# Feed-forward products on 2x2 blocks, seven block products in place of eight

## The reference, cut to what matters

```python
def ffn_block(x, hist, p):
    hu = rmsnorm(x, p['norm_ffn']) @ p['w_up']                  # 1024 -> 2 x 2816
    hp = jnp.concatenate([hist.astype(hu.dtype), hu], axis=1)
    c = lax.conv_general_dilated(hp, p['conv_w'][:, None, :], (1,), 'VALID',
                                 dimension_numbers=('NWC', 'WIO', 'NWC'),
                                 feature_group_count=hu.shape[-1]) + p['conv_b']
    a, g = jnp.split(c, 2, axis=-1)
    return x + (jax.nn.silu(a) * g) @ p['w_down'], hp[:, -(CONV_W - 1):]   # 2816 -> 1024
```

## Time and profile before

| | us |
|---|---|
| median of the runs (1861.76, 1865.08, 1868.53) | 1865.08 |
| span of the profiled execution | 1862.2 |
| `w_out`, 942.35 to 1034.68 | 92.3 |
| norm, 1034.68 to 1051.95 | 17.3 |
| feed-forward loop, 1051.95 to 1793.0 | 741.1 |
| transposes of the last rows, 1793.0 to 1815.16 | 22.2 |
| last down products and final norm, 1815.16 to 1846.19 | 31.0 |
| results, 1846.19 to the end | 16.0 |

### The profile page before, as it was taken

How to read it: one execution, slowest core, us unless ns; L and a number is a source line. 1 busy time by engine, 2 the same in 40 slices (tenths; PEclk the granted TensorE clock), 3 DMA queues, 4 the chain that set the end, 5 groups by cost and what they waited for, 6 DMA issues and landing times. The chain is left out here.

```text
span 1862.2 us, 27167 instructions
## 1 busy us (share of the span) xinstructions
PE 1730.0 (93%) x10863; PEld 1490.2 (80%) x10864; DVE 942.1 (51%) x1593; ACT 564.6 (30%) x876; POOL 351.0 (19%) x288
## 2 busy tenths in 40 slices
PE   5999999969989998878979899999999999999988
PEld 4655788956555554547979899999999999999978
DVE  3356216776553444119231455655565566556544
ACT  4001115645443444211132332222232222222232
POOL 0000100042213121212125022222222222222210
PEclk8999999979999999797989899999999999999988
DMA  6312516412326134354040111211112112111102
GB/s 241 70 63 77 222 32 227 176 57 62 102 64 214 57 93 179 119 168 148 4 128 1 42 34 40 62 34 59 42 34 68 34 34 68 34 46 55 34 12 97
DMA packets 90684, 155.15 MB, mean 83 GB/s; under 512 B 15302, under 2 KB 68078, under 8 KB 88254
## 3 DMA queue, kind: packets, MB, share of 16 engines
q1 hardware_dynamic: 76736, 93.13, 15.6%
q0 software_dynamic: 13056, 59.77, 9.8%
q10 hardware_dynamic: 816, 1.18, 0.2%
HBM read 133.61 MB, written 24.83 MB: 85 GB/s over the span
## 5 line engine op out<-in xcount | busy, mean ns | idle before, releaser
L2455 PE MATMUL ps<-h_up,w_split 128*128 128x344 f32 x2112 | 399.5, 321 | 7.1 <-DVE h_rest L2617 5.2
L2627 DVE TENSOR_TENSOR xT<-ps,xT 128x688 f32<-128x688 f32 x352 | 228.2, 690 | 283.3 <-PE ps L2455 268.3
L2455 PEld LDWEIGHTS ps<-h_up,w_split 128*128 128x128 f32 x2112 | 345.0, 189 | 8.9 <-DVE h_rest L2617 4.2
L2455 PE MATMUL ps<-gated,wd_split 128*128 128x344 f32 x1584 | 258.3, 321 | 0.9 <-ACT last_row L2569 0.9
L2455 PEld LDWEIGHTS ps<-gated,wd_split 128*128 128x128 f32 x1584 | 251.0, 188 | 1.6 <-issue 1.1
L2455 PE MATMUL ps<-h_rest,w_split 128*128 128x344 f32 x1056 | 224.8, 321 | 0.4 <-ACT wd_split L2565 0.4
L2455 PEld LDWEIGHTS ps<-h_rest,w_split 128*128 128x128 f32 x1056 | 179.1, 189 | 0.7 <-ACT wd_split L2565 0.7
L2581 POOL TENSOR_TENSOR w_split<-w_raw,w_split 128x1024 fp32r<-128x1024 f32 x44 | 114.3, 2598 | 152.4 <-ACT w_split L2527 152.4
L2541 ACT ACTIVATE hu<-ps 128x1032 f32<-128x1032 f32 x44 | 45.4, 1033 | 314.5 <-PE ps L2455 314.5
L2635 DVE SCALAR_TENSOR_TENSOR cv<-hu,ccol,cv 128x1024 f32<-128x1024 f32 x88 | 129.5, 1472 | 16.4 <-ACT cv L2543 10.7
L1719 DVE TENSOR_REDUCE top<-ps 128x1 f32<-128x384 f32 (+4 forms) x124 | 71.1, 585 | 108.1 <-PE ps L1302 63.2
(11 more groups left out here) (459 smaller groups left out, 2576.4 us busy)
## 6 DMA issues: line engine op xcount, KB each, us to landing
w_raw<-in_w_up SPq DMA_DIRECT2D x44, 512.0 KB, 6.2
wd_raw<-in_w_down SPq DMA_DIRECT2D x22, 512.0 KB, 3.6
unit<-in_cache_kv_win POOLq DMA_DIRECT2D x16, 512.0 KB, 4.5
x_kept<-xT SPq DMA_DIRECT2D x1, 4128.0 KB, 25.2
xT<-x_kept SPq DMA_DIRECT2D x1, 4128.0 KB
xtok<-in_x_prompt SPq DMA_DIRECT2D x2, 2048.0 KB, 8.2
w_qu<-in_w_in SPq DMA_DIRECT2D x2, 2048.0 KB, 8.7
w_out_sb<-in_w_out SPq DMA_DIRECT2D x4, 1024.0 KB, 11.1
```

What stands on the lines that cost most here:

```text
L2455: mm = pe.matmul(k.ps[:, bank + c, 0:TG], w(wn), x(xn)[:, c * TG:c * TG + TG], start=start and m == 0, stop=stop and m == 2)
L2627: dve.tensor_tensor(x[:, part], k.ps[:, bank + part.start:bank + part.stop, 0:TG], x[:, part], ALU.add).then_inc(added, 1)
```

## The change

The feed-forward products are made on 2x2 blocks. Up: the 8 blocks of features fall into two halves of four, the 1032 rows into two halves of 516 (HT), and the two columns are the sides a and g of step f. Strassen's scheme (in Winograd's form) needs seven block products in place of eight, of sums and differences of blocks:

- The sums of activations `S1` to `S4` are made once, ahead of the loop (S1, S2, S4 by VectorE, S3 by GpSimd), with their splits. The sums of weights `V1` to `V4` are made by GpSimd in each step (`w_sums`, four of 512 elements), and their rests and those of the raw blocks in four operations (`w_low`, three of 1024 and one of 512).
- A product is 4 blocks x 3 passes x 2 groups of 258 rows = 24 matmuls; seven of them are a step, in the order `LATER`. Products that add up share two banks (`BANK`), and A12, S3, S4 continue what A11, S2, S1 opened.
- Product A11 is copied to `base` by ScalarE. VectorE reads six results in the order u2, c11, u3, c22, c21, c12 (line 2942, 2948, 2954, 2958, 2963, 2967) into `hu`, which holds half steps z of 1032 rows as before.
- The operands are x times gain only. The norm's factor of a row is applied when PSUM is read (c11) or right behind it (`scale`, line 2971), so three products of the first step run beside the norm's sums (line 2508, 2549).
- The gated rows are stored to HBM (`g_kept`) and x with them (`x_kept_again`). The down products follow after the loop: six chunks of one or two pairs of feed-forward blocks (`CHUNKS`), four sets of output columns dp in each, seven products in a set. GpSimd makes the sums and rests of the down weights (`wd_prepare`); the sums and rests of the gated rows are made by GpSimd for pair 0 and by VectorE, piece by piece between its reads, for the others (`g_piece`). In chunk 0 ScalarE copies five of seven products out (`copies`) and stores the last rows, transposed in between (`keep_last`); afterwards VectorE adds each into `acc` (`read`) and, later, x.
- The final squares are taken in the last chunk (`FINAL`), and summed by GpSimd. The loops of the feed-forward part are written out, with no loop on the chip.
- `w_out` loads its weights block by block, and writes its sums to HBM as well.

The core of the diff; TensorE first, then ScalarE, GpSimd, VectorE:

```diff
+    LATER = ((A11, B11), (S1, V1), (S2, V2), (A12, B21), (S3, V3), (A22, V4), (S4, B22))
+    BANK = {A11: 0, A12: 0, S2: 2, S3: 2, S1: 4, S4: 4, A22: 6}
+    OPENS, CONTINUES = (A11, S2, S1, A22), (A12, S3, S4)
...
+    DOWN = ((A11, D11, 0), (S2, D2, None), (S1, D1, 4), (A12, D21, 0), (S3, D3, None), (S4, D22, 4), (A22, D4, None))
...
+    COPIED = (R_A11, R_S2, R_S1, R_A12, R_A22)
...
+    LAST_GROUPS = {0: range(0, 5), 2: range(5, NL)}
+    FINAL = [(20 + dp, d, r) for dp in range(4) for d, r in ((dp + 4, R_S4), (dp, R_A22))]
...
+            def keep_gated(f):
+                sp.wait_ge(multiplied, f + 1)
+                sp.dma_start(g_kept[f], k.cv[:, 1]).then_inc(gated_out, 16)
...
+                if f:
+                    keep_gated(f - 1)
+                if f + 2 < NF:
+                    sp.wait_ge(done, at_done(f, A12))
+                    load_up(f + 2, 0)
+                    sp.wait_ge(done, 7 * f + 7)
+                    load_up(f + 2, 1)
...
-                up(f, 0, first, f * 8 - 1, {KD - 2: ((left, f * 2), (added, f * 16)), KD - 1: ((w_upper, f * 3 + 2), (w_rest, f * 3 + 2))})
-                pe.wait_ge(gated_rest, f)
-                down(0)
-                pe.wait_ge(left, f * 2 + 1)
...
+                        for c in range(2):
+                            mm = pe.matmul(k.ps[:, bank + c, 0:HQ], ws[f % 2][:, w, a, :], xs[block][:, a, c * HQ:(c + 1) * HQ],
+                                           start=(block in OPENS and a == 0 and m == 0),
+                                           stop=(a == 3 and m == 2), skip_group_check=block in CONTINUES)
+                mm.then_inc(done, 1)
...
+                if block == A11 and f == 0:
+                    pe.wait_ge(o_added, KD - 1)
+                elif block == A11:
+                    pe.wait_ge(took, 6 * (f - 1) + C_11)
+                elif block == S1 and f:
+                    pe.wait_ge(took, 6 * (f - 1) + C_12)
...
+                elif block == A12:
+                    pe.wait_ge(based, f + 1)
...
+                elif block == S3:
+                    pe.wait_ge(took, 6 * f + U_2)
...
+                elif block == S4:
+                    pe.wait_ge(took, 6 * f + C_22)
...
+                                mm = pe.matmul(k.ps[:, bank + h, 0:HQ], ws[n % 2][:, w, m, :], xs[slot][:, block, h * HQ:(h + 1) * HQ],
+                                               start=(r <= R_S1 and m == 0 and y == 0),
...
+                act.wait_ge(w_in[f % 2], 32 * (f // 2 + 1))
+                if f >= 2 and n == 0:
+                    act.wait_ge(done, 7 * (f - 1))
+                if n:
+                    act.wait_ge(w_sum, 4 * f + W_SUMS[n])
+                g = W_GROUPS[n]
+                act.activation(group(k.w_up[f % 2], g), group(k.w_raw[f % 2], g), ACT.Copy).then_inc(w_upper, 1)
...
+            def base(f):
+                act.wait_ge(done, at_done(f, A11))
+                if f:
+                    act.wait_ge(took, 6 * (f - 1) + U_3)
...
+                act.activation(pair(k.base[:]), two(0), ACT.Copy).then_inc(based, 1)
...
+                act.wait_ge(scaled, 2 * f + z + 1)
+                if f:
+                    if z == 0:
+                        act.wait_ge(multiplied, f)
+                    else:
+                        act.wait_ge(gated_out, 16 * f)
+                act.activation(k.cv[:, z], k.hu[:, z, 2:], ACT.Identity, bias=k.ccol[:, 3, z * NF + f:z * NF + f + 1],
+                               scale=k.ccol[:, 2, z * NF + f:z * NF + f + 1]).then_inc(begun, 1)
...
+            for f in range(NF):
+                if f:
+                    base(f)
+                    silu(f - 1)
+                if f < LAST:
+                    for n in range(4):
...
+                begin(f, 0)
...
+                begin(f, 1)
...
+                for r in COPIED:
+                    act.wait_ge(down, 7 * n + r)
...
+                    act.activation(pair(dst), two(bank), ACT.Copy).then_inc(copied, 1)
+                    if r == R_A11 and n == 0:
+                        silu(LAST)
+                    if r == R_S1 and n in LAST_GROUPS:
+                        for x in LAST_GROUPS[n]:
+                            keep_last(x)
...
+                    if dp < 2:
+                        for x in range(4):
+                            g_high(1 + dp, x)
...
+            def w_sums(f):
+                w = k.w_raw[f % 2]
+                pool.wait_ge(w_in[f % 2], 32 * (f // 2 + 1))
+                if f >= 2:
+                    pool.wait_ge(done, 7 * (f - 1))
+                raw = lambda b: w[:, b]
+                for n, (o, a, b, op) in enumerate(((V1, V3, B11, ALU.subtract), (V2, V1, B22, ALU.subtract),
+                                                   (V3, B22, V3, ALU.subtract), (V4, B21, V2, ALU.add))):
+                    if n:
+                        pool.wait_ge(w_sum, 4 * f + n)
+                    pool.tensor_tensor(raw(o), raw(a), raw(b), op).then_inc(w_sum, 1)
...
+            def w_low(f, n):
+                if n == 0:
+                    pool.wait_ge(w_sum, 4 * f + 4)
+                pool.wait_ge(w_upper, 4 * f + n + 1)
+                g = W_GROUPS[n]
+                pool.tensor_tensor(group(k.w_rest[f % 2], g), group(k.w_raw[f % 2], g), group(k.w_up[f % 2], g).bitcast(F32),
+                                   ALU.subtract).then_inc(w_split, 1)
...
+            for f in range(NF):
+                if f:
+                    note(f - 1, 0)
+                    note(f - 1, 1)
+                if f < LAST:
+                    w_sums(f + 1)
+                    for n in range(4):
+                        w_low(f + 1, n)
...
+                    dve.wait_ge(convolved, 2 * f)
+                    dve.wait_ge(begun, 2 * f)
+                dve.tensor_tensor(pair(hu[:, 1, T_1]), two(2), pair(k.base[:]), ALU.add).then_inc(took, 1)
...
+                dve.tensor_tensor(pair(hu[:, 0, T_1]), two(0), pair(k.factor[:, 0:HT]), ALU.mult).then_inc(took, 1)
...
+                dve.tensor_tensor(pair(hu[:, 0, T_2]), two(2), pair(k.base[:]), ALU.add).then_inc(took, 1)
...
+                dve.tensor_tensor(pair(hu[:, 1, T_2]), two(4), pair(hu[:, 0, T_2]), ALU.add).then_inc(took, 1)
...
+                dve.tensor_tensor(pair(hu[:, 0, T_2]), two(6), pair(hu[:, 0, T_2]), ALU.add).then_inc(took, 1)
...
+                dve.tensor_tensor(pair(hu[:, 1, T_1]), two(4), pair(hu[:, 1, T_1]), ALU.add).then_inc(took, 1)
...
+            def scale(f, z, part, signal):
+                half = slice(0, HT) if part == T_1 else slice(HT, TOK)
+                ins = dve.tensor_tensor(hu[:, z, part], hu[:, z, part], k.factor[:, half], ALU.mult)
+                if signal:
+                    ins.then_inc(scaled, 1)
...
+            for f in range(NF):
+                if f:
+                    u2(f)
+                    gate(f - 1)
...
+                c11(f)
+                u3(f)
+                c22(f)
+                c21(f)
+                dve.wait_ge(took, 6 * f + C_21)
+                scale(f, 0, T_2, True)
+                scale(f, 1, T_2, False)
+                tap(f, 0, 0)
+                c12(f)
+                dve.wait_ge(took, 6 * f + C_12)
+                scale(f, 1, T_1, True)
+                tap(f, 0, 1)
+                tap(f, 1, 0)
+                tap(f, 1, 1)
...
+                    dve.tensor_tensor(raw(o), raw(a), raw(b), op).then_inc(g_sum, 1)
...
+                    dve.tensor_tensor(group(k.g_rest[s], g), group(k.g_raw[s], g), group(k.g_up[s], g).bitcast(F32), ALU.subtract
+                                      ).then_inc(g_split, 1)
...
+                dve.tensor_tensor(pair(dst), two(down_bank(n, DOWN[r - 1][2])), pair(dst), ALU.add).then_inc(joined, 1)
...
+                    read(n, r)
+                    if c < end and (dp > 0 or r >= 6) and pieces:
+                        g_piece(*pieces.pop(0))
...
+                    dve.wait_ge(x_in, 16 * d + 16)
+                    dve.wait_ge(*read_by(n, R_A22))
+                    dve.tensor_tensor(k.acc[:, d], k.acc[:, d], k.x_again[:], ALU.add).then_inc(x_joined, 1)
+                    dve.wait_ge(x_joined, d + 1)
```

972 lines of the change are left out of this document (617 added, 355 removed).

## The result

The changed kernel takes **1860.2 us** (median of 19 runs, 1852.5 to 1865.2) against 1864.8 in the runs beside it: a ratio of 0.9977, 95% interval 0.9966 to 0.9988. So it is faster by 0.23%, less than the 0.3% that I had called measurable. The forecast was 1849, 0.86% faster. The profiled execution has a span of 1856.7 us, 3.5 under its median, where before it was 1862.2.

What follows compares the result with a forecast made beforehand. TensorE, busy 93% of the span, was taken to bound the kernel. Terms from w_out on summed to 904 us against 919.9, 16 less: span 1846, plus 2.9 to the median, 1849; range 1795 to 1912.

Steps and rivals of the forecast that it cites:

- The matmul: Feed-forward matmuls on TensorE: 120 ns each at 258 columns, 5544 of them in 665 us, 85 us less than before.
- Rivals 4 and 5: Feed-forward matmuls: narrow ones bring nothing, +380 us (chance 0.01); or a matmul's fixed part goes, 1809 us (chance 0.05).
- The lock: Up loop: VectorE and GpSimd take turns at SBUF, 20.6 us of lock time a step against TensorE's 20.2.
- my layout: One up step laid out: u2 ends at 13.45 us, stalls before S1 0.4 and S3 1.45, step 22.2 us.
- The rest: Stages from the start of w_out to the span's end, summed term by term: 904 us against 919.9 before.
- w_out, 3 us: w_out: 92.3 us as now, plus 3 us for waits at d = 6 and 7, range 0 to 12.
- Five chunks, 22 us of stalls: Down stage after its first chunk: 201.6 us of matmuls plus 22 us of stalls, range 5 to 45.
- Tail, 5.2 us: Final read, square, 9 sums and root after the down stage: 5.2 us for the 9.3 before.
- 21 steps x 22.2: Up loop after its first step: 21 steps of 22.2 us, 466 us in all.
- The first chunk: First chunk of the down stage: ScalarE's serial work sets its pace, 54 us plus 8 for the clock, 62; 50 to 80.
- Within 0.3%: Whole kernel: its time changes by no more than about what a measurement can tell; chance 0.09.
- rival 3: Down stage: ScalarE's chain in the first chunk at 80 and VectorE's pieces at 30, +26, so 1875 us; chance 0.10.

Runs made afterwards that it cites:

- e1: Changed kernel with GpSimd's eight operations on the up weights cut to 8 elements each in the loop, output not the reference's: 1833.8 us, one run.
- e11: Changed kernel with GpSimd's first sum of 512 elements made twice in every step: ratio 1.0119 to the kernel before the change.
- e10: Changed kernel with the two notes of a step (10 elements each) moved from GpSimd to ScalarE: ratio 0.9985 to the kernel before the change.
- e14: Changed kernel with edits combined: w_out order, sample taps once, notes on ScalarE, first down chunk's buffers and order, pieces spread, final squares early: 1826.9 us, ratio 0.9771.
- e6: Changed kernel with the a side's second tap and the gate moved behind the next step's u2, and silu behind the weight copies: ratio 1.0244 to the kernel before.
- e2: Changed kernel with the taps of the eight sample rows made once, beside w_out: ratio 0.9949 to the kernel before the change.
- e3: Changed kernel with w_out's history transposes ahead of its first product and GpSimd's first up-weight sums and rests spread out: ratio 0.9943 to the kernel before.
- e4: Changed kernel with ScalarE making the next set's upper down weights ahead of this set's copies in the first down chunk: ratio 0.9982 to the kernel before.

## Why the prediction was wrong, point by point

**The matmul was right.** 120 ns at 258 columns was taken, and 120.7 measured where nothing waits (e1). Rivals 4 and 5 are out. The Trainium skill (TensorE: Matmul & The Clock Gate, Back-to-back issue gap) would have 110 for it by the rule that the prediction used, which the page gives for the isolated gap; the measurement decides.

**The lock was right, and its price a step a little high.** Forecast were a step of 22.2 us, a wait ahead of S3 for u2 and one ahead of S1 for c12. It is 21.4, with the wait ahead of S3 alone. In my layout u2 ended 13.45 us into the step; it ends at 12.6. The four collisions laid out ahead of it are there, at 1.0 to 1.1 us each in place of 1.15, and c12 ends at 2.6 and not at 3.2, in time for S1.

**What sets the step stays open in part.** e1 shows that it is GpSimd's operations beside VectorE that make it longer than 20.3 us. Two pictures are left of how. One is a sum: in the changed kernel an operation of VectorE with only SBUF operands, or one of GpSimd, runs for 20.7 of 21.4 us a step (by the timeline of 14 steps), close to the 20.6 estimated, and the 0.7 left is for the most part a PSUM read. It is the same in e11 (21.9 of 22.7), e10 (20.7 of 21.4) and e14 (20.4 of 21.1), so there is no gap to fill. The other is a chain of VectorE's row and the operations of GpSimd that it meets. e11 (1.28 us of GpSimd more, 1.25 us of step more) fits both. e10 took the notes' time off the sum and gave nothing, which speaks for the chain. In e6 the engines ran for 21.1 of 23.9 us, so order costs time that the sum doesn't have. e2 and e14 gave 0.24 and 0.36.

**The step that failed is "The rest", in four of its terms.**

- *w_out, 3 us, measured 10 over before.* I wrote "92.3 us as now" for TensorE's work, though the order of TensorE shown ahead of the prediction has the history's transposes gone from the norm. They stand in `w_out` now, and the sum put them at nothing: 2.9 us, and 1.6 of low clock behind them. GpSimd's place ahead of `wo_low` I had seen at d = 6 and 7; it costs 2.4 + 2.0 and not 1.2 each. The four sums took 6.41 us and not 4 x 1.26: three took 1.3 each, but the first 2.3, beside an operation of VectorE, which is the lock again. The second time it is two rests, begun late. e3 takes both away and gets 9.1 us back.
- *Five chunks, 22 us of stalls, measured 32.* The third sets' wait (3.4 to 3.9 us each in four chunks, 15 in all) is the one forecast. Left out were VectorE's three additions of the common part in each set of the last chunk. Alone they are hidden (2.45 us); in the last set they meet GpSimd's additions of squares and cost 5.2, and 2.0 more by the lower clock behind the pause. I priced the lock in the loop and forgot it here. No term had the clock either: the first 6.0 us of these chunks are at the lower level, 28 matmuls, 2.6 us more than at the full one. The rest, some 7 us, is in smaller waits.
- *Tail, 5.2 us, measured 8.0.* I read the 54 instructions of the earlier trace rows as six groups of sums, but each of the nine sums of a group is two instructions, so they are three groups. Nine sums were counted for the new tail, and there are three groups of them again, in 54 instructions: 6.7 us of TensorE.
- *21 steps x 22.2, measured 7 under.* The 19 steps from the third to the second last took 407.1 us, 15 under 19 x 22.2. The second and the last took 51.5, 7 over 2 x 22.2: the waits of 3.2 us for c12 and of 5.6 for the first down weights' rests stand at the loop's ends, where nothing was laid out.

**The first chunk came out at the 62 of the sum, in part by luck.** ScalarE's chain was named as what sets its pace, but e4 changed its order and gained nothing: the ring of weight buffers, which the prediction didn't have, was as long.

**What this did to the chances.** Loop and first step came out 8 us better than the forecast and the rest 20 us worse. "Within 0.3%" had been given 0.09. No rival had it: I had put rival 3 (the down stage) at +26, and it was +10, with `w_out`'s +7 beside it. In the range given for `w_out`, 0 to 12, the measured 10 lies near the end; I took 3 because each single wait looked small.

## What to carry to other kernels

A scheme that saves multiplications adds sums, and on this chip they are paid by two engines that take turns. Add up the time of all operations with only SBUF operands on VectorE and on GpSimd together, for each stage and not only for the longest one, and compare it with TensorE's. Here it was 20.6 against 20.2 us a step. The collisions cost 1.15 us a step by e1, some 22 us over 19 steps (an estimate) of the 85 that the matmuls were to save, and the forgotten additions of the last set 7 more. And when an operation disappears from one place of an engine's order, find where it has gone, and price it there: that is what the order is for.

## What the runs showed of the hardware

- A matmul of 258 columns follows the one before after 120.7 ns, one of 344 after 157.8: 37 ns for 86 columns, which would leave a fixed part of about 9 ns (an estimate).
- A VectorE operation on eight elements takes 0.22 us alone and 1.25 beside a row of GpSimd sums, as if it waited for one of them. It goes the other way too: in e1 GpSimd's sum of eight elements takes 0.20 us alone and 1.1 to 1.2 beside a tap of 1024. Reads with a PSUM operand took 0.68 to 0.70 us beside GpSimd's rests.
- On VectorE, three additions of 516 elements took 2.45 us with GpSimd idle for the first 1.0 of them and 7.80 beside its additions of 1032; three of GpSimd's took 2.63 to 2.67, where the like in `w_out` took 2.40 to 2.43. The smaller operations lose by far the more.
- Near the limit a step isn't constant: most of e14's steps alternate between 20.2 and 21.9 us, with waits for u2 and for c12 that come and go (5.2 and 3.6 us between 1125 and 1440 us).
